# Key and query products of two heads on all four 64x64 tiles, with token transposes moved to other banks

## The reference, cut to what matters

```python
def step(s, inp):
    w_t, k_t, v_t, a_t, b_t = inp[:5]
    sa = jnp.einsum("bhvk,bhk->bhv", s, a_t)
    s = s * w_t[:, :, None, :] + sa[..., None] * b_t[:, :, None, :] + v_t[..., None] * k_t[:, :, None, :]
    y = jnp.einsum("bhvk,bhk->bhv", s, inp[5]) if emit else None
    return s, y
```

## Time and profile before

| | |
|---|---|
| median of 3 runs | 2402.28 us (2399.34 to 2405.32) |
| the profiled execution | 2405.38 us |
| its span, first to last instruction | 2403.5 us |
| PE busy | 2314.6 us, 96% of the span |
| DVE, ACT, POOL busy | 50%, 48%, 57% |
| the chain that ended last | 87% PE, 2% DVE, 1% ACT |
| granted TensorE clock, mean | 0.99 of full speed |
| the eight pairs | from 174.9 to about 783 us |

### The profile page before, as it was taken

How to read it: one execution, slowest core, us unless ns; L and a number is a source line. 1 busy time by engine, 2 the same in 40 slices (tenths; PEclk the granted TensorE clock), 3 DMA queues, 4 the chain that set the end, 5 groups by cost and what they waited for, 6 DMA issues and landing times.

```text
span 2403.5 us, 59617 instructions
## 1 busy us (share of the span) xinstructions
PE 2314.6 (96%) x23140; PEld 1977.4 (82%) x23140; DVE 1207.1 (50%) x2359; ACT 1165.7 (48%) x1947; POOL 1368.4 (57%) x574
## 2 busy tenths in 40 slices
PE   4889999999999999999999999999999999999997
PEld 1577877787777888889999888888888888888886
DVE  1357777777775333365556455454444543333332
ACT  3234444545453444443444565555665555555554
POOL 1132233122222444458888877877887877877786
PEclk8999999999999999999999999999999999999999
DMA  9821122112111222237677555554554555555553
GB/s 390 332 99 55 58 66 69 37 57 74 64 40 57 89 88 94 99 136 267 237 257 256 186 171 175 175 174 158 174 180 164 181 175 167 177 171 175 175 183 132
DMA packets 100549, 361.39 MB, mean 150 GB/s; under 512 B 11136, under 2 KB 14336, under 8 KB 99744
## 3 DMA queue, kind: packets, MB, share of 16 engines
q1 hardware_dynamic: 99472, 357.90, 43.4%
q10 hardware_dynamic: 912, 1.03, 0.2%
HBM read 356.79 MB, written 2.10 MB: 149 GB/s over the span
## 4 chain that ended last, share of the span: by engine, by line
PE 87%; DVE 2%; ACT 1%; issue 1%; DVEq 0%; ACTq 0%
PE ps L206 27%; PE ps L207 13%; PE ps L179 6%; PE ps L181 6%; PE ps L180 6%; PE ps L584 5%; PE ps L586 3%; PE ps L585 3%; PE ps L723 2%; PE ps L701 1%; PE ps L686 1%; PE ps L853 1%; PE ps L824 1%; PE ps L728 1%; PE ps L842 1%
## 5 line engine op out<-in xcount | busy, mean ns | idle before, releaser
L170 POOL TENSOR_TENSOR wlo<-raw,whi 128x1024 fp32r<-128x1024 f32 x566 | 1364.8, 2425 | 1016.1 <-ACT whi L160 976.0
L206 PE MATMUL ps<-acts,whi 128*128 128x512 f32 x2560 | 910.3, 400 | 1.4 <-DVE acts L2575 1.4
L160 ACT ACTIVATE whi<-raw 128x1024 fp32r<-128x1024 f32 x566 | 596.4, 1055 | 314.0 <-PE ps L181 136.9
L207 PE MATMUL ps<-acts,wlo 128*128 128x256 f32 x2560 | 713.8, 279 | 0.0
L206 PEld LDWEIGHTS ps<-acts,whi 128*128 128x128 f32 x2560 | 480.7, 188 | 113.3 <-DVE acts L2575 1.7
L207 PEld LDWEIGHTS ps<-acts,wlo 128*128 128x128 f32 x2560 | 482.2, 188 | 0.9
L179 PE MATMUL ps<-acts,whi 128*128 128x256 f32 (+1 forms) x1088 | 328.0, 301 | 0.0
L181 PE MATMUL ps<-acts,wlo 128*128 128x256 f32 (+1 forms) x1088 | 324.9, 299 | 0.0
L180 PE MATMUL ps<-acts,whi 128*128 128x256 f32 (+1 forms) x1088 | 324.7, 298 | 0.0
L584 PE MATMUL ps<-acts,whi 128*128 128x512 f32 (+1 forms) x576 | 227.9, 396 | 2.9 <-issue 2.0
L179 PEld LDWEIGHTS ps<-acts,whi 128*128 128x128 f32 x1088 | 208.0, 191 | 8.3 <-issue 2.3
(11 more groups left out here) (355 smaller groups left out, 3116.0 us busy)
## 6 DMA issues: line engine op xcount, KB each, us to landing
raw<-stream SPq DMA_DIRECT2D x566, 512.0 KB, 3.3
W<-stream SPq DMA_DIRECT2D x64, 512.0 KB, 8.8
graw<-stream SPq DMA_DIRECT2D x32, 512.0 KB, 4.7
W<-xT SPq DMA_DIRECT2D x2, 2048.0 KB, 18.7
XR<-xT SPq DMA_DIRECT2D x16, 128.0 KB, 5.2
outT<-XR SPq DMA_DIRECT2D x4, 512.0 KB, 3.3
cns<-consts SPq DMA_DIRECT2D x1, 1056.0 KB, 9.7
cns<-consts SPq DMA_DIRECT2D x1, 896.0 KB, 7.2
```

The lines of the kernel that those rows point to most:

```text
L160: nc.scalar.activation(whi[slot], raw[slot], ACT.Copy).then_inc(hi_done, 1)
L170: nc.gpsimd.tensor_tensor(wlo[slot], raw[slot], whi[slot].bitcast(F32), ALU.subtract).then_inc(lo_done, 1)
L206: nc.tensor.matmul(both_parts, whi[slot][:, k, :], hl[:, :, k0 + k, :], start=first and k == 0, stop=False)
L207: ins = nc.tensor.matmul(ps[:, bank, 0:T], wlo[slot][:, k, :], hl[:, 0, k0 + k, :], start=False, stop=last and k == UK - 1)
```

## The change

It does four things.

1. `keys` is called once, at level 2, for both heads, and `queries` once for each direction at levels 3 and 4, again for both heads; in both, the head is the innermost loop. Head 0 writes bank 7, head 1 bank 0 (`PAIRED`). Level 1 has no products any more.
2. The token transposes go to columns 128 to 255 of banks 2 to 5, one block of 128 to a bank, between the copy of Y and `grown`: they wait for `y_ev`, and `grown` waits for their copy (`tokens_out`). At level 5 one fill stands ahead of them instead of behind.
3. ACT copies the tokens of a level between the two copies of `turn`, not behind both.
4. DVE masks the keys of both heads at level 2 and none at level 1; the masked queries are copied in four pieces of 256 columns instead of two of 512.

```diff
+        PAIRED = (7, 0)
...
-            def keys(h):
-                for d in range(2):
-                    for c in range(8):
-                        ins = nc.tensor.matmul(ps[side(c % 2), 7, cell(d, c // 4, c // 2 % 2)],
-                                               KA[side(h), d, chunk(c)], AL[side(h), d, chunk(c)], start=True, stop=True)
+            def keys():
+                for d, c, h in itertools.product(range(2), range(8), range(2)):
+                    ins = nc.tensor.matmul(ps[side(c % 2), PAIRED[h], cell(d, c // 4, c // 2 % 2)],
+                                           KA[side(h), d, chunk(c)], AL[side(h), d, chunk(c)], start=True, stop=True)
                 ins.then_inc(R["prod_k"].sem, 1)
 
-            def queries(h):
+            def queries(d):
                 for kind, vec in enumerate((BE, KA)):
-                    for d in range(2):
-                        for c in range(4):
+                    for c in range(4):
+                        for h in range(2):
                             o = ((d * 2 + kind) * 2 + c // 2) * C
-                            ins = nc.tensor.matmul(ps[side(c % 2), 7, o:o + C], vec[side(h), d, chunk(c)],
+                            ins = nc.tensor.matmul(ps[side(c % 2), PAIRED[h], o:o + C], vec[side(h), d, chunk(c)],
                                                    RHO[side(h), d, chunk(c)], start=True, stop=True)
                 ins.then_inc(R["prod_q"].sem, 1)
...
             def turned(vec):
                 for t in range(4):
-                    ins = nc.tensor.transpose(ps[:, 7, P * t:P * t + P], vec[:, P * t:P * t + P], ident)
+                    ins = nc.tensor.transpose(ps[:, 2 + t, P:2 * P], vec[:, P * t:P * t + P], ident)
                 return ins
...
+            def tokens_out(lv):
+                if lv <= 2:
+                    R["bt_ok"].wait(pe, i * 2 + lv)
+                elif lv <= 4:
+                    R["kt_ok"].wait(pe, i * 2 + lv - 2)
+                else:
+                    R["vt_ok"].wait(pe, i + 1)
+
+            def products(lv):
+                if lv == 2:
+                    if i:
+                        R["lnv"].wait(pe, i)
+                    keys()
                 elif lv == 3:
                     R["ev_mk"].wait(pe, i * 2 + 2)
...
                     R["rho_ok"].wait(pe, i + 1)
                     queries(0)
                 elif lv == 4:
-                    R["kt_ok"].wait(pe, i * 2 + 2)
+                    R["ev_q"].wait(pe, i * 4 + 2)
                     queries(1)
...
                 turn(lv, 0)
                 fill(1)
+                R["y_ev"].wait(pe, i * 9 + lv * 2)
                 to_tokens(lv)
                 turn(lv, 1)
...
                 fill(1)
+                tokens_out(lv)
                 apart(pe)
...
             merged_last()
             turn(LEVELS, 0)
+            fill(1)
+            R["y_ev"].wait(pe, i * 9 + 9)
             to_tokens(LEVELS)
-            fill(1)
             turn(LEVELS, 1)
...
             turned(2, 0)
+            token_beta(1)
             turned(2, 1)
-            token_beta(1)
             turned(3, 0)
-            turned(3, 1)
...
-                if lv <= 2:
-                    R["prod_k"].wait(dve, i * 2 + lv)
-                    masked(MK, 7, lv - 1, strict, "ev_mk")
-                else:
+                if lv == 2:
+                    R["prod_k"].wait(dve, i + 1)
+                    for h in range(2):
+                        masked(MK, PAIRED[h], h, strict, "ev_mk")
+                elif lv > 2:
                     queried(lv - 3)
```

More of the change, by code:

```diff
@@ L727, in turned @@
                 for t in range(4):
-                    ins = nc.tensor.transpose(ps[:, 7, P * t:P * t + P], vec[:, P * t:P * t + P], ident)
+                    ins = nc.tensor.transpose(ps[:, 2 + t, P:2 * P], vec[:, P * t:P * t + P], ident)
                 return ins
             def to_tokens(lv):
[L732 to L736, removed]
+                if lv <= 2:
+                    turned(BE[:, lv - 1, :]).then_inc(R["bt_mm"].sem, 1)
+                elif lv <= 4:
+                    turned(KA[:, lv - 3, :]).then_inc(R["kt_mm"].sem, 1)
+                else:
+                    R["conv_v"].wait(pe, i * 12 + 12)
+                    turned(vc).then_inc(R["vt_mm"].sem, 1)
+            def tokens_out(lv):
+                if lv <= 2:
+                    R["bt_ok"].wait(pe, i * 2 + lv)
+                elif lv <= 4:
+                    R["kt_ok"].wait(pe, i * 2 + lv - 2)
+                else:
+                    R["vt_ok"].wait(pe, i + 1)
[4 more added lines that the diff above has]
+                    keys()
                 elif lv == 3:
                     R["ev_mk"].wait(pe, i * 2 + 2)
[L739 to L742, removed]
-                else:
[L744 to L756, removed]
                     R["rho_ok"].wait(pe, i + 1)
@@ L801, in pe_inverse @@
             turn(LEVELS, 0)
+            fill(1)
+            R["y_ev"].wait(pe, i * 9 + 9)
             to_tokens(LEVELS)
-            fill(1)
             turn(LEVELS, 1)
             R["bon_ok"].wait(pe, i + 1)
+            R["ev_q"].wait(pe, i * 4 + 4)
             nc.tensor.matmul(ps[:, 0, 0:T], headw, bon, start=True, stop=True).then_inc(R["bonus_mm"].sem, 1)
@@ L998, in token_beta @@
                 R["bt_mm"].wait(act, i * 2 + d + 1)
[L999 removed]
+                nc.scalar.activation(tok1[:, 512 * d:512 * d + 512].rearrange("p (c f) -> p c f", c=4),
+                                     ps[:, 2:6, P:2 * P], ACT.Copy).then_inc(R["bt_ok"].sem, 1)
             def token_key(d):
                 R["kt_mm"].wait(act, i * 2 + d + 1)
[L1003 removed]
+                nc.scalar.activation(tok2[:, 512 * d:512 * d + 512].rearrange("p (c f) -> p c f", c=4),
+                                     ps[:, 2:6, P:2 * P], ACT.Copy).then_inc(R["kt_ok"].sem, 1)
             if i:
@@ L1045, in act_inverse @@
             R["vt_mm"].wait(act, i + 1)
-            nc.scalar.activation(VT, ps[:, 7, :].rearrange("p (c f) -> p c f", c=4), ACT.Copy).then_inc(R["vt_ok"].sem, 1)
+            nc.scalar.activation(VT, ps[:, 2:6, P:2 * P], ACT.Copy).then_inc(R["vt_ok"].sem, 1)
             turned(5, 1)
```

20 lines of the change are left out of this document (10 added, 10 removed), and 2 rows, old and new, of the table names.

## The result

The changed kernel takes 2410.75 us (median of 20 runs, 2402.85 to 2416.19), the kernel before 2403.62 (20 runs on the same chip, 2397.39 to 2409.22). The ratio is 1.0028, 95% interval 1.0018 to 1.0039: slower by about 7 us, where I had forecast 8 us less. The profiled execution after has a span of 2410.8 us, that of before 2403.5.

The account below looks back on a forecast made before the run. PE's own stream, busy 96% of the span, was taken as the bound. Seven steady pairs at -1.09 us (-7.6) and pair 0 at -0.45 gave -8.1 us, so a median of 2394.2 us, range 2387 to 2402.

Parts of the forecast that it names:

- Products at the four-tile rate: Keys and queries on PE: 0.95 us for the keys, 0.475 per queries call, 1.82 us less in a pair.
- Exposed update after level 1: Level 1 to 2: `merged` waits for DVE's update of X, starting at 1.24 instead of 0.95, 0.29 us lost.
- before `merged_last`: Level 4 to 5: `merged_last` needs both update halves, ready at 1.67 against PE's 1.43, 0.24 us lost.
- 0.2 us for Y at level 3: Token transposes at level 3 wait for Y's copy behind DVE's two key masks: 0 to 0.25 us lost, 0.2 taken.
- Copies of tokens out of four banks: ACT's token copy from four banks was taken to last 0.60 us, with an upper end of 1.1 us.
- the slower rival: ACT's four-bank copy takes 0.9 us or more and delays `grown`; at 1.5 us, 2413 us in all; chance 0.08.
- The arithmetic of the sum: Steady pair: products -1.82, update waits +0.29 and +0.24, wait for Y +0.2, giving -1.09 us.
- each burst counts by the step from its start to that of the next: PE's own stream is the bound, so each burst on PE costs its start-to-start step.
- the rival of no gain: Keys miss the four-tile rate (2406 us), or PE has one more 1.1 us issue gap per pair (2403.0); chance 0.20.
- Cost nothing: `grown`'s wait for ACT's token copy and its place on ACT: slack of 0.4 and 0.3 us, so no cost.
- unreleased gaps over 5 us above before: Sign that the forecast is wrong: PE's unreleased gaps sum up to more than 5 us above those of before.

Follow-up runs that it names:

- e5: Kernel before with one `square` issued twice in each of the eight pairs (64 records more each): ratio 1.0093, 25.4 us slower.
- e12: e10 with the wait before `grown` for the token copy made real, the wait for Y still already met: ratio 1.0110 to the kernel before.
- e10: e8 with both added waits put on a semaphore met since the start, same instruction count: ratio 1.0010 to the kernel before.
- e8: Kernel before plus ACT's new copy order and both new waits (token transposes for Y, `grown` for token copy), tokens still in bank 7: ratio 1.0041.
- e6: Changed kernel with products as before (one head a call, bank 7), tokens in banks 2 to 5 with new waits and ACT order: 1.0033 to kernel before.
- e9: Kernel before with paired products in banks 7 and 0, tokens still in bank 7, no token copy wait before `grown`: ratio 1.0035.
- e18: Changed kernel with each key and query product writing its 64 columns twice and every second product left out: ratio 0.9971 to the kernel before.
- e19: e9 with each key and query product writing its 64 columns twice and every second product left out: ratio 0.9989 to the kernel before.
- e1: Changed kernel with 128 one-instruction markers at PE's start: ratio 1.0028 to the kernel before.
- e3: Changed kernel with the head as outermost loop of keys and queries, so they run on two tiles: ratio 1.0035 to the kernel before.
- e13: e9 with one fill moved from behind level 5's transposes to between `grown` and the keys of level 2: ratio 1.0036 to the kernel before.
- e17: Kernel before with each key and query product writing its 64 columns twice and every second product left out: ratio 0.9977.
- e2: Kernel before with 128 one-instruction markers at PE's start: ratio 0.9998.

## Why the prediction was wrong

By its own steps:
- *Products at the four-tile rate*: right, 0.96 and 0.50 us against 0.95 and 0.475: 64 records in 0.96 us are 15 ns each.
- *Exposed update after level 1*: 1.21 against 1.24, right; *before `merged_last`*: 1.78, against 1.67 forecast; *0.2 us for Y at level 3*: not there, M3 to G3 even fell by 0.08.
- *Copies of tokens out of four banks*: 598 ns on average, as taken; the slower rival's mechanism didn't occur, and `grown` doesn't wait for ACT in a pair's steps.
- Undisturbed, a pair is 1.22 us shorter, against 1.09. The arithmetic of the sum was right, with two terms off by 0.2 and 0.1 us in opposite directions.
- *The step that failed* is the assumption under the sum, that "each burst counts by the step from its start to that of the next", with PE's issue gaps left as they were. I had seen the gaps and priced them inside the rival of no gain, at one more gap of 1.1 us a pair, without asking what makes them. As I read them, they are set by the supply of instructions: they stand at 192 to 194 beyond a multiple of 256 and end 1.4 us (median) after a packet, and 64 records more in the squares cost 3.2 us where the array needs 1.0 (e5). So array time saved inside a dense stretch is given back at its border, and the low clock behind four of the gaps adds to it: 6.8 us of clock and some 9 of gaps (the rest of the 16 of excess) against 9.8 gained.
- The second failure was to say "Cost nothing" of `grown`'s wait for the token copy, because slack of 0.4 us covered it. The array is covered; the packet isn't: against `grown` it starts 1.1 us later in e12 than in e10. This wait alone costs 21 us in e12 against e10 (24 against the kernel before); with the other wait beside it (e8) it is 11 against the kernel before.
- The condition that the prediction named, unreleased gaps over 5 us above before, is what came: 22.8 against 14.2.

How the loss divides between the copy wait and the density in the changed kernel isn't settled: either alone makes it as slow (e6, e9), and together they are no worse. Nor is it settled what still holds e18 and e19. Profiles of single executions don't help further: those of e1, e3, e9 and e13 lie 4 to 7 us under the medians of their kernels.

## What to carry to other kernels

Where PE issues hundreds of small matmuls in a row, count its instructions, not only its columns: look in the waits for gaps that nothing releases, see whether they repeat at a fixed count of instructions and end at a fixed time after an instruction packet, and price the stretch by a doubled burst, whose records you have counted in the trace, before making it denser. Here, half the instructions at the same columns gained 0.2 to 0.6% (e17 to e19, which compute other products), and the faster tile form gained nothing. A wait that is covered by work of the array can still cost if it is open when the sequencer comes to it, which in e10 was 1.5 us ahead of the array: put it as late as it may stand, and test it against a wait that is already met, with the same instructions.

## What the runs showed of the hardware

- From 170 to 800 us, 307 of 317 gaps of PE that nothing releases stand at 192 to 194 beyond a multiple of 256 instructions, counted in the traces of all kernels here, also with 128 markers in front (e1, e2). Each packet of the instruction queue has 16 KB, and at those gaps PE goes on 1.4 us (median) after one has ended.
- 64 records more in a dense stretch cost 3.2 us, 1.0 at the array's rate (e5).
- A wait for the token copy, ahead of `grown`, costs 21 us over the same instructions with waits already met (e12, e10), though PE's undisturbed steps are the same (M2 to G2 3.96 us, M3 to G3 4.06 and 4.07). The marker behind the wait is passed 0.4 us ahead of `grown` instead of 1.5, and the packet starts 1.3 us after the marker in both (pair 1, level 2).
- After a gap of 1.73 us that ended at 289.19, the granted clock is 0.57 over the next 4 us; after the one of 1.22 us that ended at 276.15, L586 to L587 takes 0.23 us, the full rate. After a gap of 2.00 us in the kernel before (336.74) it stays at 1.00.
- The copy of 128 columns from each of four banks takes 0.60 us, as one of 512 columns from one bank.
